# Five raw slots with low halves over raw weights, rounding and subtraction one unit further ahead, and a mixed order at two layer boundaries

## The reference

```
# first block, four layers
mkv = mem @ w_mem_kv                       # 256 memory rows, keys and values of 4 heads
h = layer_norm(x)
for kind in (a, b, c, a):
    proj = h @ w_in_kind
    branch = a: real part of a 2-D FFT over tokens and 256-wide groups of h
             b: 16 query heads, 4 kv heads, rms-normed and rotated, softmax attention
             c: 3 groups of 16 heads, dilated windows (1, 4, 16), merged by log-sum-exp
    y = concat(branch, memory_attention(qm, mk, mv)) * silu(gate)
    h = layer_norm(8 ** 0.25 * h + y @ w_out)
# second block, two layers
for l in (0, 1):
    h = rmsnorm(x); uv, z, xbc, dt, c_q, c_kv, k_rope = split(h @ w_in)
    mix = concat(gmlp(uv), ssd(z, xbc, dt), mla(c_q, c_kv, k_rope))
    x = x + mix @ w_out
    x = x + square(relu(rmsnorm(x) @ mlp_w1)) @ mlp_w2
return rmsnorm(x)
```

## Time and profile before

| | us |
|---|---|
| median of three runs (lowest, highest) | 1285.99 (1285.71, 1286.32) |
| profiled execution, its own time | 1284.71 |
| profiled execution, span | 1282.9 |
| PE busy | 1244.9 |
| DVE busy | 892.5 |
| ACT busy | 704.9 |
| granted clock of PE, mean | 0.998 |

### The profile page before, as it was taken

One profiled execution on the slowest core, in us unless ns is written; L12 is line 12 of the kernel. 1 busy time (PEld: TensorE's weight loads), 2 busy tenths in 40 slices (PEclk: granted clock), 3 DMA queues, 4 the chain that ended last, 5 costly groups with the idle time before them and its releaser, 6 DMA issues.

```text
span 1282.9 us, 19007 instructions
## 1 busy us (share of the span) xinstructions
PE 1244.9 (97%) x7448; PEld 1064.4 (83%) x7448; DVE 892.5 (70%) x1604; ACT 704.9 (55%) x1031; POOL 2.4 (0%) x8
## 2 busy tenths in 40 slices
PE   9999999999999999999999999999999999999997
PEld 8997787778888787877988987888888987888885
DVE  6677996684664746548567998766657998766655
ACT  5635577444467566575536676544444676544442
POOL 0000000000000000000000000000000000000000
PEclk9999999999999999999999999999999999999999
DMA  8444432544644434333353544465654544456560
GB/s 285 158 162 137 160 128 71 165 164 164 224 138 132 131 102 163 98 131 120 115 181 95 175 142 139 157 197 178 213 168 149 155 155 133 142 189 204 186 224 33
DMA packets 147119, 197.61 MB, mean 154 GB/s; under 512 B 4541, under 2 KB 102103, under 8 KB 147031
## 3 DMA queue, kind: packets, MB, share of 16 engines
q1 hardware_dynamic: 146902, 196.35, 46.9%
q0 software_dynamic: 128, 0.04, 0.0%
HBM read 195.33 MB, written 1.05 MB: 153 GB/s over the span
## 4 chain that ended last, share of the span: by engine, by line
PE 77%; DVE 13%; ACT 6%; issue 3%; DMA 1%; SPq 0%; DVEq 0%; ACTq 0%
PE bank L506 18%; PE bank L508 17%; PE bank L507 17%; PE bank L1532 9%; PE bank L1533 5%; PE bank L594 4%; DVE w_lo L2207 3%; DVE stat L2227 2%; ACT w_hi L1638 1%; PE bank L819 1%; PE bank L1105 1%; PE bank L1142 1%; DMA w_raw<-in_w_mem_kv 1%; DVE stat L2224 1%; DVE arena L2221 1%
## 5 line engine op out<-in xcount | busy, mean ns | idle before, releaser
L2207 DVE TENSOR_TENSOR w_lo<-w_raw,w_hi 128x2048 fp32r<-128x2048 f32 (+5 forms) x189 | 410.6, 2182 | 139.4 <-ACT w_hi L1638 136.9
L1638 ACT ACTIVATE w_hi<-w_raw 128x2048 fp32r<-128x2048 f32 (+5 forms) x189 | 344.5, 1829 | 222.1 <-PE bank L508 152.0
L506 PE MATMUL bank<-w_hi,r_hi 128*128 128x512 f32 (+3 forms) x536 | 207.7, 387 | 1.5 <-DVE w_lo L2207 1.3
L508 PE MATMUL bank<-w_hi,r_lo 128*128 128x512 f32 (+3 forms) x536 | 204.2, 381 | 0.0
L507 PE MATMUL bank<-w_lo,r_hi 128*128 128x512 f32 (+3 forms) x536 | 204.0, 381 | 0.0
L1532 PE MATMUL bank<-h_both,w_hi 128*128 128x512 f32 x512 | 181.6, 399 | 2.0 <-DVE h_both L3011 2.0
L506 PE MATMUL bank<-w_hi,h_both 128*128 128x512 f32 (+3 forms) x464 | 178.1, 384 | 1.9 <-DVE w_lo L2207 1.1
L508 PE MATMUL bank<-w_hi,h_both 128*128 128x512 f32 (+3 forms) x464 | 174.6, 376 | 0.0
L507 PE MATMUL bank<-w_lo,h_both 128*128 128x512 f32 (+3 forms) x464 | 174.4, 376 | 0.0
L1533 PE MATMUL bank<-h_both,w_lo 128*128 128x256 f32 x512 | 143.5, 280 | 0.0
L506 PE MATMUL bank<-h_both,w_hi 128*128 128x256 f32 x464 | 133.9, 289 | 2.3 <-DVE w_lo L2207 2.1
(11 more groups left out here) (322 smaller groups left out, 1598.1 us busy)
## 6 DMA issues: line engine op xcount, KB each, us to landing
w_raw<-in_mlp_w SPq DMA_DIRECT2D x64, 1024.0 KB, 5.3
w_raw<-in_w_out SPq DMA_DIRECT2D x24, 1024.0 KB, 5.0
w_raw<-in_w_in_c SPq DMA_DIRECT2D x48, 512.0 KB, 4.5
w_raw<-in_w_in_c SPq DMA_DIRECT2D x18, 1024.0 KB, 5.0
w_raw<-in_w_in_a SPq DMA_DIRECT2D x12, 1024.0 KB, 6.8
w_raw<-in_w_in_b SPq DMA_DIRECT2D x12, 1024.0 KB, 5.1
w_raw<-in_w_in SPq DMA_DIRECT2D x8, 1024.0 KB, 5.8
w_raw<-in_w_out SPq DMA_DIRECT2D x8, 512.0 KB, 3.7
```

The costliest lines, as they stand in the source:

```text
L506: nc.tensor.matmul(o, lhs[0], rhs[0], start=start, stop=False)
L508: return nc.tensor.matmul(o, lhs[1], rhs[0], start=False, stop=stop)
L1638: nc.scalar.activation(w_hi[:, u % SPLIT_SLOTS, 0:kts * n], w_raw[:, u % RAW_SLOTS, 0:kts * n], ACT.Copy).then_inc(w_rounded.sem, w_rounde ...
L2207: v.tensor_tensor(w_lo[:, s, 0:m], w_raw[:, u % RAW_SLOTS, 0:m], w_hi[:, s, 0:m].bitcast(F32), ALU.subtract)\
```

## The change

- `w_lo` has no buffer of its own any more: the subtraction writes over the raw weights in the same slot. The raw buffer, now `w_low`, has five slots (`RAW_SLOTS`), `w_hi` four (`SPLIT_SLOTS`); together nine slots of 8 KB per partition, as before.
- Load u waits for the product of unit u−5 instead of the subtraction of unit u−3. The first five loads are issued without a wait.
- `NEAR, FAR = 3, 4` replace the look-aheads of 2 and 3 wherever these were the defaults or were written as `SPLIT_SLOTS - 1` and `SPLIT_SLOTS`. Calls with fixed numbers keep them, but for two at each layer's end: the rounding at `(wo,1,0)` and `out_stats(1,0)` look two ahead instead of one.
- At the boundaries a0 to b0 and b0 to c0, PE turns tiles 0 and 1 of row half 1 after six k's, and tiles 2 and 3 after all eight. ACT's `normal_rows` of half 1 come after tile j = 3 of half 0. The rounding there comes at tile j = 2 of row half 1 and is that of unit 16 (34). DVE does `half_lo(0, 2)` before `row_norm` of half 1, and no subtraction behind it.

```
-RAW_SLOTS = 3
-SPLIT_SLOTS = 3
+RAW_SLOTS = 5
+SPLIT_SLOTS = 4
+NEAR, FAR = 3, 4
...
-        w_raw = sb("w_raw", [P, RAW_SLOTS, UNIT])
+        with nc.sbuf_tensor("w_raw", [P, RAW_SLOTS, UNIT], F32) as w_raw:
+            pass
+        w_low = sb("w_low", [P, RAW_SLOTS, UNIT], F32R)
         w_hi = sb("w_hi", [P, SPLIT_SLOTS, UNIT], F32R)
-        w_lo = sb("w_lo", [P, SPLIT_SLOTS, UNIT], F32R)
+        def w_lo(u, part=slice(0, UNIT)):
+            return w_low[:, u % RAW_SLOTS, part]
...
                         for k in range(4):
+                            if (b, kh, k) == (0, 1, 2):
+                                turn_rows(before, 1, (0, 1))
...
                             unit_done[u] = keys[b]
+                            if b == 0:
+                                turn_rows(before, 1, (2, 3))
                         elif b == 1:
...
-                        else:
-                            turn_rows(before, 1)
...
-            for u in range(RAW_SLOTS, N_UNITS):
-                sp.wait_ge(w_split.sem, w_split.at(u - RAW_SLOTS))
+            for u in range(3, N_UNITS):
+                if u >= RAW_SLOTS:
+                    sp.wait_ge(product_done.sem, product_done.at(unit_done[u - RAW_SLOTS]))
                 load_unit(u)
...
-            def round_weights(key, ahead=SPLIT_SLOTS):
+            def round_weights(key, ahead=FAR):
...
-                    if j == 3 and not fourier:
-                        normal_rows(L, 1, 0)
-                        normal_rows(L, 1, 1)
...
                         half_hi(nxt, 0, 1, tiles_read)
-                        round_weights((L, "zt", 1, 0), 1)
-                if fourier:
-                    normal_rows(L, 1, 0)
-                    normal_rows(L, 1, 1)
+                normal_rows(L, 1, 0)
+                normal_rows(L, 1, 1)
                 for j in range(4):
...
+                    elif j == 2:
+                        round_weights((L, "zt", 1, 0), 1)
                     half_hi(nxt, 1, j, tiles_read)
...
-                round_weights((L, "wo", 1, 0), 1)
+                round_weights((L, "wo", 1, 0), 2)
...
-            def weights(key, ahead=SPLIT_SLOTS - 1):
+            def weights(key, ahead=NEAR):
...
-                    v.tensor_tensor(w_lo[:, s, 0:m], w_raw[:, u % RAW_SLOTS, 0:m], w_hi[:, s, 0:m].bitcast(F32), ALU.subtract)\
+                    v.tensor_tensor(w_lo(u, slice(0, m)), w_raw[:, u % RAW_SLOTS, 0:m], w_hi[:, s, 0:m].bitcast(F32), ALU.subtract)\
...
-                    product((L, "zt", b, j), 1)
+                    product((L, "zt", b, j), 0 if b == 1 and nxt[0] != "a" else 1)
...
-                out_stats(L, 0, 0, SPLIT_SLOTS - 1)
-                out_stats(L, 1, 0, 1)
+                out_stats(L, 0, 0, NEAR)
+                out_stats(L, 1, 0, 2)
...
-                if nxt[0] == "a":
-                    half_lo(0, 2)
+                half_lo(0, 2)
                 row_norm(L, 1, factor=ALPHA)
-                weights((L, "zt", 1, 0), 1)
-                if nxt[0] != "a":
-                    half_lo(0, 2)
                 half_lo(0, 3)
```

More of the change, by code:

```diff
@@ L501, in unit @@
                 slot, (_, kts, n) = u % SPLIT_SLOTS, source
-                return u, [w[:, slot, 0:kts * n].rearrange("p (k n) -> p k n", k=kts) for w in (w_hi, w_lo)]
+                return u, [w.rearrange("p (k n) -> p k n", k=kts) for w in (w_hi[:, slot, 0:kts * n], w_lo(u, slice(0, kts * n)))]
             def mm3(o, lhs, rhs, start, stop):
@@ L748, in _ @@
             units.append(rows_of(A["w_mem_kv"], 0, KT, 0, MEM_W))
-            first = [w[:, 0, 0:KT * MEM_W].rearrange("p (k n) -> p k n", k=KT) for w in (w_hi, w_lo)]
+            first = [w.rearrange("p (k n) -> p k n", k=KT) for w in (w_hi[:, 0, :], w_lo(0))]
             for kh in range(2):
@@ L1777, in gate_silu @@
                     def gate_silu(u):
-                        round_weights((L, "gate", u), SPLIT_SLOTS - 1)
+                        round_weights((L, "gate", u), NEAR)
                         act.wait_ge(product_done.sem, product_done.at((L, "gate", u)))
@@ L1928, in heads @@
                             if q is None:
-                                round_weights((L, "xt", *turned, 0), SPLIT_SLOTS - 1)
+                                round_weights((L, "xt", *turned, 0), NEAR)
                             turn(*turned)
@@ L1974, in _ @@
                     qk_section(3)
-                    round_weights((L, "gate", 2), SPLIT_SLOTS - 1)
+                    round_weights((L, "gate", 2), NEAR)
                     act.wait_ge(product_done.sem, product_done.at((L, "gate", 2)))
@@ L1980, in _ @@
                         pair_turned(q - 1)
-                        round_weights((L, "t", q - 1, 1), SPLIT_SLOTS - 1)
+                        round_weights((L, "t", q - 1, 1), NEAR)
                         pair_exp(q)
@@ L1994, in _ @@
                     normal_rows(L, 0, 0)
-                    round_weights((L, "wo", 1, 1), SPLIT_SLOTS - 1)
+                    round_weights((L, "wo", 1, 1), NEAR)
                     normal_rows(L, 1, 1)
@@ L2206, in weights, with product @@
                     dve.wait_ge(w_rounded.sem, w_rounded.at(u))
-                    v.tensor_tensor(w_lo[:, s, 0:m], w_raw[:, u % RAW_SLOTS, 0:m], w_hi[:, s, 0:m].bitcast(F32), ALU.subtract)\
+                    v.tensor_tensor(w_lo(u, slice(0, m)), w_raw[:, u % RAW_SLOTS, 0:m], w_hi[:, s, 0:m].bitcast(F32), ALU.subtract)\
                         .then_inc(w_split.sem, w_split.next(u))
-            def product(key, ahead=SPLIT_SLOTS - 1):
+            def product(key, ahead=NEAR):
                 weights(key, ahead)
@@ L2330, in normal_half, with gated @@
                 v.tensor_scalar(z[:, 1, 0:512], src, S_(154, 1), S_(9, 1), SUB, MUL).then_inc(rows_normal_v.sem, rows_normal_v.next(L))
-            def gated(L, j, key, src, parts=range(3), ahead=SPLIT_SLOTS - 1):
+            def gated(L, j, key, src, parts=range(3), ahead=NEAR):
                 t, pair = split_t[:, 0, :], slice(2 * j, 2 * j + 2)
@@ L2418, in _ @@
                     for g in range(4):
-                        product((L, "f1", g, 1), SPLIT_SLOTS - 1 - j)
+                        product((L, "f1", g, 1), NEAR - j)
                         o = bank[f1_bank(j, g, 1)][:, 0:2 * HALF].rearrange("p (s k) -> p s k", s=2)
@@ L2441, in _ @@
                         key = (L, "mo") if of == 4 else (L, "f2", of)
-                        weights(key, SPLIT_SLOTS if of == 3 else SPLIT_SLOTS - 1)
+                        weights(key, FAR if of == 3 else NEAR)
                         dve.wait_ge(gate_read.sem, gate_read.at((L, "gate", of)))
@@ L2543, in _ @@
                     heads_out(len(B_PAIRS) - 3)
-                    weights((L, "t", 8, 1), SPLIT_SLOTS)
+                    weights((L, "t", 8, 1), FAR)
                     heads_out(len(B_PAIRS) - 1)
@@ L2603, in heads_out @@
                     def heads_out(j, key, parts=range(3)):
-                        weights(key, 0 if j == 3 else SPLIT_SLOTS - 1)
+                        weights(key, 0 if j == 3 else NEAR)
                         if j == 2:
@@ L2608, in heads_out @@
                             dve.wait_ge(gate_ready.sem, gate_ready.at((L, "late" if j == 3 else "early")))
-                        gated(L, j, key, bank[C_OUT_BANK][:, :], parts, ahead=0 if j == 3 else SPLIT_SLOTS - 1)
+                        gated(L, j, key, bank[C_OUT_BANK][:, :], parts, ahead=0 if j == 3 else NEAR)
                     def heads(*at):
@@ L2618, in heads @@
                                 pair_max(q)
-                            weights((L, "s", q, 1), SPLIT_SLOTS)
+                            weights((L, "s", q, 1), FAR)
                             if q:
@@ L2680, in _ @@
                         if j == 1:
-                            weights((L, "wo", 1, 1), SPLIT_SLOTS - 1)
+                            weights((L, "wo", 1, 1), NEAR)
             def add_rows(key, n, b, o, factor=None):
@@ L2998, in tile_scaled @@
                 def tile_scaled(part, gain, j):
-                    product((part, "zt", j), SPLIT_SLOTS - 1 if j < 2 else 1)
+                    product((part, "zt", j), NEAR if j < 2 else 1)
                     if j >= 2:
```

20 lines of the change are left out of this document (10 added, 10 removed).

## The result

The changed kernel takes 1298.12 us (median of four runs, 1296.29 to 1299.86), the kernel before 1285.94; the ratio is 1.0097, 95% interval 1.0084 to 1.0109. Predicted were 1287.1 us, range 1281.5 to 1291.5.

The account below looks back on a forecast made before the run. PE was taken to bound the kernel, busy 1244.9 of 1282.9 us. The terms 0.8 + 0.45 − 0.25 + 0.4 − 0.3 = +1.1 us, added to the median 1285.99, gave 1287.1 us, 80% range 1281.5 to 1291.5.

Parts of the forecast that it names:

- Slots: Weight slots in steady work: loads released by product u−5 keep a margin of 0.15 to 0.45 us; costed at nothing.
- The test that I set: Sign of a wrong forecast in the profile after: ACT L1638 waiting on DMA over 10 us in sum, meaning late loads.
- Startup: Start of the kernel: loads 3 and 4 issued at once, nothing moved by more than 0.3 us; taken as 0.
- Boundaries: a0 to b0 and b0 to c0: first product to second half takes 7.1 instead of 8.45 us, gain 1.35 each.
- b0: At weights((s,0,1)) two subtractions fall together, delaying the turned q that PE waits for; net +0.8 us, bounds −2.2 and +2.3.
- First rope of c0: Three subtractions instead of two ahead of rope(0,0), which PE waits for; +0.45 us, bounds −1.35 and +2.3.
- c0 steady: Steady part of c0: each call subtracts one unit, only another one; 0, with 2.6 us all there is to win.
- End of c0: Smaller subtraction ahead of the gating gains 1.9 at most, c0 to a1 boundary moves; −0.25 us, bounds −1.9 and +1.
- MLP fronts and MLPs: d0 and d1: two subtractions ahead of add_rows cost +0.2 at each front; steady MLP work counts −0.3 for both.
- loads come late: Slower rival: ACT waits in round_unit for loads in c0; +7, 1294 us, half of them 1290.5; chance 0.23.
- the deeper look-ahead does nothing: PE waits only 4.4 us for low halves and five of seven waits stay; 1286 to 1287, with the sum chance 0.50.
- show whole: Case that the extra subtractions delay PE by their full length, +2.3 twice or thrice; within the slower chance of 0.23.

Follow-up runs that it names:

- kernel with old look-aheads: The changed kernel with `NEAR, FAR = 2, 3` as before, keeping the new slots and mixed boundary order; 1282.87 us, ratio 0.9976.
- the hold: The changed kernel with the look-ahead of before at all places where its trace shows a new wait of PE, q = 0 in c0 included; 1286.58 us.
- kernel with the gates held: The changed kernel, but ACT's rounding behind each silu of a gate in the two fourier layers looks three ahead instead of four; 1296.07 us, ratio 1.0079.
- kernel with the longer wait: The kernel before, with DVE making the subtraction of unit 35 twice and half of that of unit 75 twice; 1290.96 and 1293.18 us.

## Why the prediction was wrong

*Slots: right.* They cost nothing (1284.42 alone). The test that I set, ACT waiting over 10 us for loads, came out against me, though: ACT L1647 waits 35 us for loads in the changed kernel (L1638 4.4 before), with landings up to 7.0 us behind the start (unit 53). But nothing hangs on most of these waits, and the kernel with old look-aheads, which is faster, has 26.5 us of them. The test was badly chosen; the step holds except at the start. Most groups of 1 MB loads took 5.0 to 5.2 us in the median, as the earlier trace rows said, and not the 4.4 us that one gets, as an estimate, from the fit in the Trainium skill's "DMA: Bandwidth & Descriptors"; that fit is for DMAs that GpSimd issues, and these are issued by SP. But the prediction read two groups only. Another on the same page of the kernel before is slower, and it is the one of the start:

```profile
w_raw<-in_w_in_a SPq DMA_DIRECT2D x12, 1024.0 KB, 6.8
```

*Startup: wrong.* The step "my walk moves nothing by more than 0.3 us" failed. The default look-ahead behind the first silu draws in unit 7 ahead of the first spectrum's copies, while its load is still on its way (9.2 us from issue to landing, as before, when it was not yet wanted): 1.9 us, and 0.9 at a second place in a0 and in a1, 3.7 us together. I had looked at what the changed calls need from DVE, not at when the loads of the start land.

*Boundaries: right.* From first product to second half PE takes 122.64 − 115.68 = 6.96 us, forecast 7.1, before 8.45; the wait is 0.27 for 0.55 forecast.

*b0: mechanism and wait right, price wrong.* The turned q starts at 172.78, 4.19 us after the earlier trace rows; 3.43 of these were there at the boundary's start (115.68 against 112.25), so the place gives +0.76, forecast +0.8. The step that failed is the silent one under the sum: that a wait of PE costs its length and no more. PE stood 3.59 us in one piece, and 5.5 us at half clock behind it took 2.5 more. I had written down "stands until about 169.4" and never asked what a pause of three microseconds does to the clock.

*First rope of c0: the same.* 282.30 against 275.13 is 7.17, less the 6.66 with which b0's last units came, +0.51 for +0.45 forecast (the forecast's own terms give 270.4 against 265.54 + 4.49, which is +0.38); then 2.5 us of clock (measured as the further loss up to unit 36).

*c0 steady: wrong.* "Each call subtracts one unit, only another one: 0" failed at one place. The two subtractions at 363.81 and 371.25 of before stand in a row at 373.57 after, ahead of a rope: 2.3 us of wait, 1.5 of clock. That the clock part goes with the stack was not tested for this place, as the hold missed it.

*End of c0: numbers right, mechanism in part.* −1.9 at the gating, and +1.9 at c0 to a1 for +1.65. But the gating wait goes with ACT's earlier rounding alone, where I had walked it as the smaller subtraction on DVE; and 1.3 us at c0 to a1 are there with the old look-aheads too. They come from the two numbers that look two ahead at the output product, where I had put all of it down to out_stats(0,0) behind subtraction 81. That the sum of −0.25 fits is luck to that extent.

*MLP fronts and MLPs:* forecast +0.1 together; between units 84 and 189 the distance grows by 0.6 us.

The sum in the form of the prediction: 1.1 forecast; start and gates +3.7, clock behind two waits +5.0, the third stack +3.8, and the initial 0.9 of the profile make 14.5 of the 15.1 in the profile. Between the medians there are 12.2, so that one of the terms, most likely the clock's, was smaller in the other runs; which, is not shown. Of the rivals "loads come late" named the wrong place (c0, where it was the start) and "the deeper look-ahead does nothing" was too kind; that stacked subtractions "show whole" was put with the late loads and not priced as the main case. The chance of slower should have been the largest.

## What to carry to other kernels

A look-ahead that is a default in a program ordered by hand doesn't shift evenly: where calls with fixed numbers stand between default ones, one unit more is a stack of two or three at one place. Walk to the next such place and ask what stands behind the stack, and whether the loads have landed by then; deepen only where the heavy step stands ahead of a wait (here 17 units of 190 gave about 1.3 us, and two fixed numbers put back gave as much, while all 190 took 15.2). Deepen one engine at a time: near the end of c0 ACT alone took away the gating wait without stacks on DVE. And price a wait of PE that grows to 2.3 us or more at its growth plus up to 2.5 us of clock, for here the clock mostly halved behind it.

## What the runs showed of the hardware

PE's granted clock fell to 0.50, the level of 1.2 GHz, at each wait of 2.3 to 3.6 us in two profiles of the changed kernel (six of six), and at three waits of 6.68 us. Over all profiles, their start and end left out, it fell at 19 of 20 waits of 2.29 us or more. How long it stayed low differs for the same wait: at those of 3.6 us 6.8 us in the changed kernel, of which PE worked 5.2 to 5.9, and 3.4 us in the kernel with the gates held; at those of 2.3 us 3.4 us every time. It is no fixed rule of length: a wait of 3.84 us was followed by full clock once and by a dip once in the same kernel, one of 1.94 us at the start by none, one of 1.40 to 1.42 us at c0 to a1 by a dip in some kernels and by none in the kernel before. What decides there stays open. The Trainium skill, "TensorE: Matmul & The Clock Gate", part 1, says that the number of matmuls at the low clock at a kernel's start differs from run to run; the two runs of the kernel with the longer wait, where the dip came and went, fit that. The four executions of the changed kernel differ in mean clock as in time (0.991, 0.993, 0.995, 0.996 at 1299.86, 1298.38, 1297.86, 1296.29 us), so its scatter of 3.6 us against 0.6 before is likely the same effect; only one of the four has a trace, so it is not shown.
